# An expert gather ring that runs on over stage boundaries, in a one-core decoder-layer kernel

## The chip, the cores and the metric

The kernel runs on one core of a Trainium2 chip. The metric is the device time of one execution in microseconds. The program is one launch.

## The reference, cut to what matters

One layer of a hybrid decoder for 1104 tokens of 1024 features: 16 learned meta tokens and 1024 prompt tokens in sequence, and 8 samples of 8 tokens that start from given states. All in float32.

```python
h = layer_norm(x)
proj = h @ w_in                     # q, k, v, gates, SSM inputs, two gates z
o = gated_delta_chunked(...)        # 16 heads; a triangular solve in each chunk
y = ssd_chunked(...)                # 16 heads
h1 = layer_norm(ALPHA * h + concat(o, y) @ w_out)
# PEER: for each token, 8 heads pick 16 experts each out of 16384, by two top-16 lists of 128 keys
act = gelu(einsum('thkd,td->thk', u_tab[idx], h1))
ff = einsum('thk,thkd->td', gate * act, v_tab[idx])
y_out = layer_norm(ALPHA * h1 + ff)
```

Every token needs 128 rows of `u_tab` and 128 rows of `v_tab`, 4 KB each. These rows are gathered out of HBM, and they are most of the bytes that the kernel moves.

## The kernel before, in words

**Tiles.** The tokens lie in eight tiles of 128 (tiles 0 to 7) and a last tile of 80 (64 sample tokens and 16 prompt tokens).

**Stages.** The program (L2516) is a series of stages. Each is a block of its own with its own semaphores, and all engines meet in a barrier behind it. A stage of the kind `project` (L130) makes the input projection of two to four tiles; `mix_tile` (L1001) does the two recurrent mixers, the output projection and the choice of experts for one tile. The names here: P1 (tiles 0, 1), M0, M1, P2 (tiles 2 to 4), M2, M3, M4, P3 (tiles 5 to 7 and the last), M5, M6, M7, ML (the last tile), F (the experts of the last tile, `experts_folded`, L2317), and a short stage that stores states.

**The experts run beside the stages.** The work on the experts of tile t is laid over the stages behind Mt. It has two kinds of units. A u unit gathers row n of the choices of all 128 tokens (128 rows of 4 KB, one on each partition, L2122); VectorE multiplies it by the tokens and sums (L2158). A v unit gathers the 128 v rows of one token (L2122 too); TensorE adds them, weighted, to two banks of PSUM, for four tokens at a time with 16 matmuls (L2274), whose weights ScalarE copies into a strip (L2235). When a tile has all of its v units, VectorE normalises it (`normalize`, L2168), and a DMA stores it. `tail` means v units of a tile whose v units began in the stage before, `head` those that begin in this stage after its u units have been turned into weights (`tensor_turn`, L2282). The stages M2 and M5 have no u units: each works off all 128 tokens of tile 1 or of tile 4.

**The ring.** All gathers are issued by GpSimd and land in a ring of 12 slots of 512 KB (`RING`, L783). Slot g mod 12 has one semaphore, `in{g mod 12}`. Before it issues unit g, GpSimd waits until unit g - 12 is used up (`freed`, L2088): a u unit by VectorE's `dot`, a v unit by TensorE's `v_used`, which counts groups of four, a stored tile by its DMA.

**The order.** `order` (L2024) lays the units of a stage over its checkpoints by written weights (`SHARES` L904, `project_points` L118), and every engine works them off at the same checkpoints of its own program. GpSimd runs 12 units ahead. In a mix stage it waits first for two small loads (`consts`, L1137), which SyncE issues fourth and fifth, and casts a mask (L1138); in a project stage it waits for three loads (L276).

**The end of a stage.** Behind its last unit GpSimd waits until every slot has landed, sets `gathered`, and resets the DMA semaphores:

```python
for i in range(RING):
    if self.landings[i]:
        g.wait_ge(S[f"in{i}"], 16 * self.landings[i])
g.sem_inc(S["gathered"], 1)
g.dma_reset(range(min(nums), max(nums) + 1))
```

In a mix stage VectorE waits for `gathered` before it copies the new choices (L2209). The block ends with a barrier; `all_engine_barrier(sems_to_clear=S.range)` is a second one, in which GpSimd clears the semaphores of the stage. The ring and its counts begin at slot 0 again in the next stage. ScalarE takes the strips of the last checkpoint before it computes the softmax's exponentials (L1649 to L1653).

## Time and profile before

| | us |
|---|---|
| median of 3 runs | 4942.41 |
| lowest and highest | 4938.36, 4945.6 |
| profiled execution, first to last instruction (span) | 5061.9 |

For the profiled execution no time is given other than its span, 119.5 us (2.4%) above the median. The stages start at 559.7 (M1), 946.1 (P2), 1332.8 (M2), 1668.1 (M3), 2067.1 (M4), 2509.2 (P3), 2993.0 (M5), 3324.0 (M6), 3720.2 (M7), 4151.5 (ML) and 4796.2 (F) in the span. In rows PE is TensorE, PEld its weight loads, DVE VectorE, ACT ScalarE, POOL GpSimd, SPq the issues of SyncE; `e_ring` is the ring, `e_ff` the two banks of PSUM.

### The profile page before, as it was taken

What the parts mean: (1) busy time and instruction counts of PE and PEld (TensorE: products, weight loads), DVE (VectorE), ACT (ScalarE), POOL (GpSimd) and SP (SyncE); (2) the same over time, 40 slices, a digit from 0 to 9 for tenths busy, and PEclk for the clock granted to TensorE, in tenths of its full rate; (3) what the DMA queues carried; (4) which work ended last, traced back from release to release, by engine and by line L of the source; (5) the groups of instructions that cost most, each with busy time, mean ns of one, the idle gap of its engine ahead of it and who ended that gap; (6) DMA issues with size and microseconds to landing.
All of it is one profiled execution on the core that took longest, in us unless ns stands there. A gap on an engine that the chain in (4) does not pass through costs nothing. (4 is left out here: it accounts for less than half of the span.)

```text
span 5061.9 us, 53189 instructions
## 1 busy us (share of the span) xinstructions
PE 3427.8 (68%) x17745; PEld 1968.4 (39%) x17745; DVE 3195.1 (63%) x7030; ACT 725.4 (14%) x2596; POOL 2650.2 (52%) x2240
## 2 busy tenths in 40 slices
PE   7978377599887576556579988757656564565516
PEld 5666262255462452343144446245234322321101
DVE  5335896588544896677668744489667755664370
ACT  2141110111210210210022121021021011000000
POOL 1000376465435575676546533557567647726564
PEclk9988668699888678776789999877877776677659
DMA  5453478899859789989879875978999988879897
GB/s 180 145 192 119 175 262 327 295 368 353 322 181 366 268 314 369 336 320 335 336 271 355 307 293 167 369 275 307 368 344 321 367 317 300 303 295 361 300 370 281
DMA packets 460478, 1497.56 MB, mean 296 GB/s; under 512 B 53184, under 2 KB 115456, under 8 KB 447632
## 3 DMA queue, kind: packets, MB, share of 16 engines
q0 software_dynamic: 317952, 1141.01, 61.7%
q1 hardware_dynamic: 121040, 330.55, 17.6%
q10 hardware_dynamic: 21216, 22.60, 1.4%
q8 instruction: 145, 2.38, 0.2%
q14 instruction: 125, 1.02, 0.1%
HBM read 1455.22 MB, written 55.52 MB: 298 GB/s over the span
## 5 line engine op out<-in xcount | busy, mean ns | idle before, releaser
L2122 POOL DMA_INDIRECT e_ring<-peer_u,e_idx x1024 | 1325.0, 1294 | 647.9 <-issue 231.6
L2122 POOL DMA_INDIRECT e_ring<-peer_v,e_idxT x1024 | 1119.7, 1093 | 891.4 <-PE e_ff L2274 445.5
L2158 DVE CUSTOM_DVE_ANT_0 e_ring<-e_ring,e_x 128x1024 f32<-128x1024 f32 x1024 | 1226.5, 1234 | 291.1 <-DMA e_ring<-peer_u,e_idx 270.6
L2274 PE MATMUL e_ff<-e_ring,e_strips 128*32 128x512 f32 x4096 | 672.4, 786 | 512.0 <-DMA e_ring<-peer_v,e_idxT 429.5
L352 PE MATMUL p_ps<-p_hT,p_w 128*128 128x256 f32 (+2 forms) x1728 | 569.9, 484 | 0.0
L2274 PEld LDWEIGHTS e_ff<-e_ring,e_strips 128*32 128x32 f32 x4096 | 146.5, 129 | 933.9 <-issue 931.7
L352 PEld LDWEIGHTS p_ps<-p_hT,p_w 128*128 128x128 f32 x1728 | 329.0, 195 | 209.0 <-issue 129.5
L1138 POOL CAST hidden<-delta 128x128 bf16<-128x128 f32 (+1 forms) x9 | 2.9, 317 | 629.7 <-DMA delta<-hidden 605.7
L376 PE MATMUL p_ps<-p_w,p_hT 128*128 128x512 f32 (+1 forms) x576 | 251.2, 599 | 0.0
L1299 PE MATMUL bank<-X,atp 128*128 128x128 f32 (+1 forms) x1120 | 170.5, 304 | 102.3 <-DVE XT L1736 70.7
L1313 PE MATMUL bank<-T,XT 128*128 128x128 f32 (+1 forms) x1088 | 167.8, 304 | 93.1 <-DVE T L1744 91.4
L1911 DVE MAX8 top<-kb_kdec 128x8 f32<-128x128 f32 (+1 forms) x144 | 40.3, 280 | 301.5 <-ACT kb_kdec L1645 248.3
L1504 PE MATMUL bank<-wbuf,kqb 128*128 128x512 f32 (+1 forms) x448 | 209.8, 618 | 0.0
L614 DVE SCALAR_TENSOR_TENSOR p_y<-p_cbuf,p_cw,p_y 128x256 f32<-128x256 f32 (+2 forms) x324 | 198.3, 612 | 11.5
L1299 PEld LDWEIGHTS bank<-X,atp 128*128 128x128 f32 (+1 forms) x1120 | 149.8, 210 | 124.9 <-DVE XT L1736 79.1
L1313 PEld LDWEIGHTS bank<-T,XT 128*128 128x128 f32 (+1 forms) x1088 | 149.6, 214 | 115.6 <-DVE T L1744 101.8
L1322 PE MATMUL bank<-XT,T 128*128 128x128 f32 (+1 forms) x1120 | 160.5, 293 | 3.8 <-DVE T L1744 3.8
L376 PEld LDWEIGHTS p_ps<-p_w,p_hT 128*128 128x128 f32 (+1 forms) x576 | 108.2, 188 | 141.1 <-issue 141.1
L1322 PEld LDWEIGHTS bank<-XT,T 128*128 128x128 f32 (+1 forms) x1120 | 149.7, 210 | 4.2 <-DVE T L1744 4.2
L2235 ACT COPY e_strips<-e_wT 128x4 f32<-128x4 f32 x256 | 48.7, 204 | 688.1 <-PE e_ff L2274 394.8
L1504 PEld LDWEIGHTS bank<-wbuf,kqb 128*128 128x128 f32 (+1 forms) x448 | 83.2, 193 | 136.1 <-issue 135.2
L560 DVE COPY p_tok<-p_ps 128x384 f32<-128x384 f32 (+1 forms) x108 | 55.3, 512 | 118.1 <-PE p_ps L336 109.8
(392 smaller groups left out, 5150.1 us busy)
## 6 DMA issues: line engine op xcount, KB each, us to landing
p_w<-w_in SPq DMA_DIRECT2D x156, 512.0 KB, 3.6
wbuf<-wc SPq DMA_DIRECT2D x56, 1024.0 KB
wbuf<-w_out SPq DMA_DIRECT2D x40, 1024.0 KB
e_ring<-peer_v,e_idxT POOLq DMA_INDIRECT x1104
atp<-w_out SPq DMA_DIRECT2D x16, 1024.0 KB
kb_kdec<-w_out SPq DMA_DIRECT2D x16, 1024.0 KB
atp<-wc SPq DMA_DIRECT2D x16, 1024.0 KB
e_ring<-peer_u,e_idx POOLq DMA_INDIRECT x1024
```

The costliest lines, as they stand in the source:

```text
L352: last = nc.tensor.matmul(ps[j % 2][:, 0:cols], w[:, j % NWR, k, :], hT[:, k, :], start=(k == 0), stop=(k == KT - 1))
L376: last = nc.tensor.matmul(ps[n % 4][0:R, :], hT[:, k, col[i]:col[i] + R], w[:, slot:slot + 4, k, :], start=(k == 0), stop=(k == KT - 1))
L560: last = v.tensor_copy(tok[:, j % 2, 0:nf, :], ps[4 + m % 2][:, 0:prompt].rearrange("p (i n) -> p i n", n=P))
L614: last = v.scalar_tensor_tensor(out=y, in0=xx[:, i:i + convw], scalar=cw[:, j, i:i + 1], in1=y, op0=ALU.mult, op1=ALU.add)
L1299: last = mm(bank[b][0:R, i * P:i * P + R], atp[0:R, s, i, 0, 0:R], X[0:R, s, i, 0:R], start=True, stop=True)
L1313: last = mm(bank[b][0:R, i * P:i * P + R], XT[0:R, s, i, 0:R], T1[0:R, s, i, 0:R], start=True, stop=True)
L1322: last = mm(bank[b][0:R, i * P:i * P + R], T1[0:R, s, i, 0:R], XT[0:R, s, i, 0:R], start=True, stop=True)
L1504: last = mm(bank[2 + i][0:R, :], h1T[:, 4 * half + kk, 0:R], wtile[n + 8][:, kk * 512:(kk + 1) * 512], start=(half == 0 and kk == 0), stop ...
L2122: g.indirect_dma_start(out=self.ring[:, i % RING, :], out_offset=None, in_=table[:, :], in_offset=at, bounds_check=NEXP - 1, oob_is_err=Fa ...
L2158: v.tensor_tensor_reduce(out=self.ring[0:U, i, :], in0=self.ring[0:U, i, :], in1=self.x[0:U, :], scale=1.0, scalar=0.0, op0=ALU.mult, op1= ...
L2235: nc.scalar.copy(self.strips[:, q % NSTRIP, j:j + width, 31:32], self.wT[:, :].rearrange("p (j m) -> p j m", m=32)[:, j:j + width, s:s + 1 ...
L2274: last = nc.tensor.matmul(self.ff[i][32 * j:32 * j + 32, :], self.strips[:, self.strip_of[t] % NSTRIP, j, 31 - s:63 - s], self.ring[:, sel ...
```

## The change

- The ring is one for the whole series of stages. A `Plan` for each stage holds `base`, the number of units before it, and the landings so far of each slot; the semaphores `in0` to `in11` are never cleared between stages, and GpSimd waits no longer for its gathers at the end of a stage. `gathered` is gone.
- At the end of a stage GpSimd issues the first units of the next one, as many as are `known`: v units at the head of its order, at most 12. That is 8 before P2, 12 before M2, 4 before M3, 8 before M4, 12 before P3, 12 before M5, 4 before M6, 8 before M7 and 12 before ML, 80 in all. Each still waits for its slot.
- At the start of a stage GpSimd issues the u units that follow among the first 12 (`fresh`) before it waits for any load.
- The block and the barrier behind it go by semaphores alone, without a drain of GpSimd. SyncE clears the semaphores.
- The weights give a stage with a tail more v units at its very start: in a mix stage at `start`, in a project stage behind the transposes of each tile.
- M2 and M5 take 112 tokens instead of 128. The other 16 are the tail of M3 and of M6, so that tiles 1 and 4 are normalised and stored in the middle of M3 and M6, not at the end of M2 and M5.
- ScalarE does the exponentials before the strips of the last checkpoint.
- Code for an early turn and for a u part in pieces comes in too, and is used by no stage.

```diff
+def stage_end(nc, S):
+    nc.sync.sem_clear(S.range)
+    nc.all_engine_barrier(sem_only=True)
...
-    w = {"ln": (2, 2, 0)}
+    w = {}
+    for i in range(len(tiles)):
+        w["ln", i] = (4, 0, 0)
+    w["ln"] = (0, 2, 0)
...
-        with nc.Block() as block:
+        with nc.Block(no_gpsimd_drain=True) as block:
...
                 if peer:
+                    peer.pool_first(g)
                     at = peer.pool(g)
...
-        nc.all_engine_barrier(sems_to_clear=S.range)
+        stage_end(nc, S)
...
-    "series": {"start": (0, 0, 0), "norm": (0, 0, 0), "prep": (0, 2, 0), "raw": (3, 4, 0), "inv0": (3, 3, 0), "T": (1.6, 2, 0),
+    "series": {"start": (14, 0, 0), "norm": (0, 0, 0), "prep": (0, 2, 0), "raw": (3, 4, 0), "inv0": (3, 3, 0), "T": (1.6, 2, 0),
...
-                for e in range(EH):
+                for e in range(EH - 1):
                     at("best", e)
                 act.wait_ge(S["soft"], 1)
                 nc.scalar.activation(B["best"][0:R], B["best"][0:R], ACT.Exp).then_inc(S["exp_ready"], 1)
+                at("best", EH - 1)
...
+    def slot(self, g):
+        return (self.base + g) % RING
+
+    def known(self):
+        n = 0
+        while n < min(RING, len(self.seq)) and (self.seq[n][0] == "v" and (self.seq[n][1] < self.n_tail or not self.U) or
+                                                self.seq[n][0] == "u" and not self.starts):
+            n += 1
+        return n
+
+    def fresh(self):
+        n = self.known()
+        while n < min(RING, len(self.seq)) and self.seq[n][0] == "u":
+            n += 1
+        return n
...
     def pool_end(self, g):
+        S, p, then = self.S, self.plan, self.then
         self.pool_at()
-        S = self.S
-        for i in range(RING):
-
-            if self.landings[i]:
-                g.wait_ge(S[f"in{i}"], 16 * self.landings[i])
-        g.sem_inc(S["gathered"], 1)
-        nums = [S[f"in{i}"].num for i in range(RING)]
-        g.dma_reset(range(min(nums), max(nums) + 1))
+        if then is None:
+            return
+        for i in range(then.known()):
+            self.freed(g, len(p.seq) + i - RING)
+            self.gather(g, S, then, i)
+
+    def pool_first(self, g):
+        p = self.plan
+        for i in range(p.known() if p.base else 0, p.fresh()):
+            self.gather(g, self.S, p, i)
...
     def take_choice(self, v):
         S = self.S
-        v.wait_ge(S["gathered"], 1)
         self.copy_choice(v, S)
...
-        mix(2, head=(1, 0, P))
-        mix(3, u=2, head=(2, 0, 80))
-        mix(5, head=(4, 0, P))
-        mix(6, u=5, head=(5, 0, 80))
+            (2, dict(head=(1, 0, 112))),
+            (3, dict(tail=(1, 112, P), u=(2, 0, SLOTS), head=(2, 0, 80))),
+            (5, dict(head=(4, 0, 112))),
+            (6, dict(tail=(4, 112, P), u=(5, 0, SLOTS), head=(5, 0, 80))),
```

## Rows read from the trace of the kernel before

**Rows 1.** The page: the span, each engine's busy time, and GpSimd's DMA queue.
```profile
span 5061.9 us, 53189 instructions
PE 3427.8 (68%) x17745; PEld 1968.4 (39%) x17745; DVE 3195.1 (63%) x7030; ACT 725.4 (14%) x2596; POOL 2650.2 (52%) x2240
...
q0 software_dynamic: 317952, 1141.01, 61.7%
```

**Rows 2.** Windows, a stage each: length, then PE, PEld, DVE, ACT, POOL busy (instructions), PEclk, DMA share, GB/s.
```profile
946.10:1332.80 386.70, 334.25 (x1150) 181.91 (x1150) 296.96 (x570) 65.58 (x192) 218.03 (x176) 0.92 0.92 350
1332.80:1668.10 335.30, 250.16 (x1624) 145.67 (x1624) 161.69 (x420) 55.26 (x201) 133.09 (x130) 0.84 0.71 265
1668.10:2067.10 399.00, 259.27 (x1438) 163.88 (x1439) 303.03 (x661) 56.65 (x193) 261.08 (x210) 0.75 0.89 327
2067.10:2509.20 442.10, 278.62 (x1566) 163.59 (x1566) 312.77 (x679) 57.54 (x201) 286.09 (x242) 0.75 0.90 334
2509.20:2993.00 483.80, 413.14 (x1344) 197.04 (x1344) 330.39 (x663) 92.99 (x421) 243.41 (x192) 0.92 0.84 306
...
3324.00:3720.20 396.20, 254.22 (x1438) 159.67 (x1439) 302.84 (x661) 56.16 (x193) 263.88 (x210) 0.77 0.89 329
3720.20:4151.50 431.30, 271.74 (x1566) 158.61 (x1566) 311.74 (x679) 57.55 (x201) 288.07 (x242) 0.77 0.93 342
4151.50:4796.20 644.70, 340.38 (x1950) 147.16 (x1950) 342.01 (x752) 48.45 (x189) 377.87 (x322) 0.69 0.85 312
```

**Rows 3.** Windows around stage boundaries: into P2, into M3, into M5.
```profile
939.10:949.10 10.00, 4.10 (x29) 0.87 (x21) 0.79 (x4) 0.00 (x0) 0.00 (x0) 0.84 0.41 155
...
1650.00:1671.10 21.10, 6.18 (x29) 1.10 (x21) 14.55 (x45) 1.24 (x2) 0.00 (x0) 0.58 0.20 69
...
2957.00:2996.00 39.00, 32.09 (x76) 12.88 (x74) 14.20 (x26) 7.61 (x11) 0.00 (x0) 0.99 0.27 101
```

**Rows 4.** Waits within M4: who for whom, us in total, times, longest.
```profile
PE e_ff L2274 <- DMA e_ring<-peer_v,e_idxT: 52.1, 15, 9.0
```

**Rows 5.** Windows: 60 us of P2 with the DMA engines full.
```profile
1095.00:1155.00 60.00, 58.44 (x228) 32.79 (x227) 56.57 (x110) 11.14 (x40) 41.28 (x35) 1.00 1.03 407
```

**Rows 6.** Timeline, end of M1 and start of P2: start, length, instruction, [idle before, releaser].
```profile
936.31 0.99 POOL L2122 DMA_INDIRECT e_ring<-peer_v,e_idxT  x1 [0.30 <-DMA e_ring<-peer_v,e_idxT]
937.60 3.37 PE L2274 MATMUL e_ff<-e_ring,e_strips 128*32 128x512 f32 x16 [3.55 <-DMA e_ring<-peer_v,e_idxT]
...
942.64 1.92 PE L2274 MATMUL e_ff<-e_ring,e_strips 128*32 128x512 f32 x16 [1.67 <-DMA e_ring<-peer_v,e_idxT]
...
946.12 1.28 SPq L192 DMA_DIRECT2D p_x<-x  x3
...
956.11 0.99 POOL L2122 DMA_INDIRECT e_ring<-peer_u,e_idx  x1 [18.81 <-DMA p_bias<-ln_in_b]
```

**Rows 7.** Timeline, start of M3: the first u unit that VectorE takes.
```profile
1685.76 1.23 DVE L2158 CUSTOM_DVE_ANT_0 e_ring<-e_ring,e_x 128x1024 f32<-128x1024 f32 x1 [8.61 <-DMA e_ring<-peer_u,e_idx]
```

**Rows 8.** Timeline, end of M2 and start of M3.
```profile
1653.44 3.64 PE L2274 MATMUL e_ff<-e_ring,e_strips 128*32 128x512 f32 x16 [1.36 <-DMA e_ring<-peer_v,e_idxT]
...
1657.26 1.29 DVE L2176 BATCH_NORM_STATS2 e_stats<-e_ff 128x6 f32<-128x512 f32 x2
...
1663.67 0.28 DVE L1978 TENSOR_REDUCE norm<-best 128x8 f32<-128x128 f32 x1
...
1665.08 0.22 DVE L2204 COPY e_idxf<-pick 128x128 f32<-128x128 f32 x1
1668.14 0.33 SPq L1071 DMA_DIRECT2D rows<-rows  x1
```

**Rows 9.** Windows, M2, the v matmuls (L2274) alone: length, PE and PEld busy.
```profile
1332.80:1668.10 335.30, 77.98 (x512) 16.88 (x512) 0.84 0.71 265
```

**Rows 10.** DMA issues, size, us to landing: at the start of P3, then amid gathers.
```profile
p_x<-x SPq DMA_DIRECT2D x3, 512.0 KB, 4.6
...
p_x<-x SPq DMA_DIRECT2D x1, 320.0 KB, 6.5
```

More of the change, by code:

```diff
@@ L288, in _ @@
                 ident = B["ident"]
-                if peer:
+                if peer and peer.plan.starts:
                     peer.tensor_start(pe, ps[5])
@@ L482, in _ @@
                 n = Chain(v, S["n_v"])
-                if peer:
+                if peer and peer.plan.starts:
                     peer.vector_start(v, ps[5])
@@ L1481, in _ @@
                 at("turn")
-                if peer.U:
+                if peer.plan.turns and not peer.plan.early:
                     peer.tensor_turn(pe, bank[3])
@@ L1498, in _ @@
                     if half == 0:
-                        if i == 1 and peer.U:
+                        if i == 1 and peer.plan.turns and not peer.plan.early:
                             pe.wait_ge(S["w_taken"], 1)
@@ L1630, in _ @@
                 at("turn")
-                if peer.U:
+                if peer.plan.turns and not peer.plan.early:
                     peer.scalar_turn(act, bank[3])
@@ L1883, in _ @@
                 at("turn")
-                if peer.U:
+                if peer.plan.turns and not peer.plan.early:
                     peer.vector_turn(v)
@@ L2528, in program @@
+        plans, base, counts = [], 0, [0] * RING
+        for some, parts in stages:
+            mixed = None if isinstance(some, list) else some
+            points = project_points(some) if mixed is None else checkpoint_weights("series" if "u" in parts else "tokens")
+            plans.append(Plan(points, base, counts, mixed=mixed, **parts))
+            base, counts = base + len(plans[-1].seq), plans[-1].counts
         project(nc, io, B, [0, 1], pool_dma, consts=Constants(io, B, e))
-        e.B = B
+        e.bind(io, B, None, None)
@@ L2541, in program @@
-        experts_folded(nc, e, pool_dma)
+        for (some, _), plan, then in zip(stages, plans, plans[1:] + [None]):
+            e.bind(io, B, plan, then)
+            if plan.mixed is None:
+                project(nc, io, B, some, pool_dma, peer=e)
+            else:
+                mix_tile(nc, io, B, pool_dma, plan.mixed, e)
+        experts_folded(nc, e, pool_dma, base, counts)
         store_states(nc, io, B)
```

301 lines of the change are left out of this document (164 added, 137 removed).

## The prediction

> **What bounds the kernel now.** I read the page's head first, then windows stage by stage, then windows around the boundaries, then the timeline at three of them.
>
> The page [rows 1] shows no engine at its limit: TensorE is busy for 68% of 5061.9 us, VectorE for 63%. GpSimd's queue, which carries the gathers, moves 1141 MB and takes 61.7% of the 16 DMA engines' time by itself. Stage by stage [rows 2] it is clearer: P2, M3, M4, M6, M7 and ML run the DMA engines at 0.85 to 0.93 while TensorE is busy for two thirds or less (P2 aside). M2 is different, with a share of 0.71 in 335.3 us, and M5 does the same work for its tile. P3 has TensorE at 413 of 483.8 us. In M4 the gathers are what is waited for: TensorE stands 52.1 us before v units [rows 4]. So I call M3, M4, M6, M7 and ML bound by the gathers, M2 and M5 by the tile's own chain, P3 by TensorE, and P2 by both.
>
> The boundaries are where the DMA engines stand still [rows 3]. From the share in each window: into P2 10.0 x 0.59 = 5.9 us, into M3 21.1 x 0.80 = 16.9, into M5 39.0 x 0.73 = 28.5. The other six, read alike, give 9.6 (M2), 7.4 (M4), 7.7 (P3), 16.8 (M6), 5.8 (M7) and 7.3 (ML): 105.9 us in nine. The timeline shows why [rows 6]: GpSimd issues M1's last gather at 936.3, TensorE's last group ends at 944.6, SyncE's first load follows at 946.1 behind the barriers, and the next gather at 956.1, because GpSimd waits for loads first. The stage's end is set by TensorE's last four tokens, not by GpSimd's wait: that wait is over at about 942.7, so its removal alone is worth nothing there.
>
> All terms below are made against the profiled execution (5061.9 us) and taken as microseconds off the median of 4942.4, 2.4% shorter. At this size the difference is below 1 us.
>
> **A: 80 gathers issued before the barriers.** A gather is 128 x 4 KB = 0.524 MB. With the engines full they move 407 GB/s [rows 5], so one costs 1.29 us of DMA time, and 80 cost 103 us. At a boundary this can take no more than the idle time there, nor more than its own gathers: into P2 5.9 us, M3 5.2 (4 gathers), M4 7.4, P3 7.7, M6 5.2, M7 5.8, ML 7.3. Sum 44.5. Into M2 and M5 I count nothing: those stages don't wait for the DMA engines, and P3's end is TensorE's (32.1 us busy of 39 [rows 3]). Its last gather lies far ahead of its end. Into P2 and P3, which TensorE partly bounds, I let the full term stand because the first 8 and 12 tokens now fall where it waits for the layer norm. Bounds: 0, if the stages' own chains take over at once, and 105.9 if every idle microsecond is filled and felt. I take **-44.5**.
>
> **B: u units issued before the stage's loads land.** In M3 VectorE idles 8.6 us before its first u unit [rows 7]; M1 and M6 start alike. GpSimd's first issue moves up by about 10 us, but the stage's loads fill the DMA engines just then. Bounds 0 and 3 x 8.6 = 25.8; I take a third, **-9**, since the transfers still have to share the engines.
>
> **C: no normalisation and no store at the ends of M2 and M5.** VectorE is at 1657.3 when the normalisation begins and at 1663.7 when it is done [rows 8]; the store follows, and M3 starts at 1668.1. Without them the seven short operations from 1663.67 to 1665.30 start at 1657.3 and end at 1658.9. With the 1.6 us that the barriers take from TensorE's last matmul to SyncE's first load [rows 6], the next stage starts at 1660.5: 7.6 us earlier. TensorE's last group ends at 1657.1 and does not hold it. Twice that is **-15.2**, bounds 0 and -16.
>
> **D: 16 tokens from M2 to M3, and from M5 to M6.** M2 gets rid of 64 matmuls at 78.0/512 = 0.152 us [rows 9], 9.8 us of TensorE, and of 8 MB. I take 7 us for each stage, **-14**, bounds 0 and -19.6. M3 and M6 pay. What a token costs in such a stage comes from two pairs [rows 2]: M4 has 32 v units more than M3 and takes 43.1 us longer, M7 has 32 more than M6 and takes 35.1: 1.35 and 1.10 us, a normalisation in the middle included. For 16 tokens 21.6 and 17.5: **+39**, bounds +20 (half, if the new tokens fall into waits) and +43.
>
> **E: GpSimd comes late to the barrier.** A gather takes GpSimd 1.3 us with the gap before it (0.99 and 0.30, [rows 6]). Into P3 and ML the last four of 12 wait for TensorE's last group, so GpSimd is at the barrier 5.2 us behind it. Into P2, M4 and M7 the last four of 8 wait for the group before: at M1's end 941.0 + 5.2 = 946.2, 1.6 us behind TensorE. Together 10.4 + 4.9 = 15.3. What is queued behind the barrier is SyncE's loads and with them the whole next stage, but the DMA engines work meanwhile. Half: **+8**, bounds 0 and +15.3.
>
> **F: the loads of a stage meet gathers.** SyncE's queue is passed by up to 12 gathers. A load of 512 KB at a stage's start lands after 4.6 us, one of 320 KB amid gathers after 6.5 [rows 10], so at least 1.9 us more. Eight stages will begin with gathers in flight: M1, P2, M3, M4, P3, M6, M7 and ML (those for M2 and M5 are released by VectorE's last u units and land before): at 1.9 us 15, if the chain binds. In the gather-bound ones it mostly doesn't: **+4**, bounds 0 and +15 by these rows; how far above it could go is a rival.
>
> **G: the barrier's form.** The clearing moves from GpSimd to SyncE and stays on the path. All of a boundary's sequencing is 1.6 us [rows 6], so twelve of them are worth at most a few microseconds either way: 0, bounds -6 and +6. The earlier exponentials are covered by the last v units, which end later: 0, and 3 us a stage if that cover were gone.
>
> Sum: -44.5 - 9 - 15.2 - 14 + 39 + 8 + 4 = -31.7, which gives **4911 us**.
>
> **Rivals.**
> 1. *All idle DMA time comes back.* If the whole series, M2 and M5 included, is paced by the ring, A is up to -105.9, and with the other terms the change is -93: 4849. For it: shares of 0.9 between the boundaries. Against it: M2's share of 0.71, and P3's end, where nothing waits for a gather.
> 2. *The gain cancels.* The chain of each tile takes over where the gathers were: A falls to -20.5 (only M4, M7 and ML hold), the rest stands: -8, 4935. For it: M3, M6 get work and M2, M5 have room left. The change not doing what it says belongs here: if the new barriers still wait for GpSimd's DMAs, A is gone, and E grows by the flight of 12 gathers.
> 3. *Slower: the loads at the start.* The place is the first 10 us of eight stages, the mechanism the sharing of the DMA engines: 12 gathers are 15.5 us of DMA time, and the rows and gates that a mix stage starts with are 2.4 MB, 6 us. Every microsecond that these land later starts the tile's chain later. From 31.7/8 = 4 us above F's half microsecond on, it decides. At 8 us a stage the change is +28: 4970. For it: 6.5 us for the smaller load [rows 10]. Against it: in gather-bound stages the chain has the slack of its waits [rows 4].
>
> On rival 3 the Trainium skill has a rule (DMA: Bandwidth & Descriptors, Queues, rings and completion order): each DMA engine takes turns between the queues that have work, a packet at a time. By it the 2.4 MB wait for at most as many bytes of gathers, an estimate of 6 us a stage and not 15, and the sum would be about 48 us higher at most, 4955: slower, by the rule's worst case. The rows show 1.9 us and more, and I go by them.
>
> **How the numbers follow.** A measurement of this kernel can tell about 0.2%, 10 us, from no change. The forecast (-10 to -65 us) gets 0.58, rival 1 (beyond -65) 0.14, rival 2 (within 10 us) 0.16, rival 3 0.12. So faster 0.72, same 0.16, slower 0.12. The likeliest case's own range is 4877 to 4932. The range that should hold 8 in 10 goes from 4852, most of rival 1, to 4950, most of rival 2 and the near end of rival 3.
>
> **What would show it.** A: DMA idle at the boundaries into P2, M3, M4, M6, M7 and ML down from 5.8 to 7.7 us to 2 or less, and v matmuls at the start of M4 before the tile's own. B: VectorE's idle before the first u unit of M3 below 6 us. C: M2 and M5 shorter by about 15 us each. D: M3 and M6 no more than 15 us longer than now. E: GpSimd's last gather ends after TensorE's last group at the ends of M4 and M7. F: the first load of M4 lands within 7 us. The forecast is wrong if M4, M7 and ML, which keep their units, don't get shorter by 5 us or more each, or if M2 and M5 stay at 330.

## The result, and the profile after

| | us |
|---|---|
| before, median of 17 runs | 4941.07 (4929.36 to 4950.74) |
| after, median of 17 runs | 4956.71 (4944.22 to 4969.1) |
| ratio after to before | 1.0032, 95% interval 1.0021 to 1.0042 |
| profiled execution of after, span | 4962.1 |

The change makes the kernel slower by 0.32%, 16 us; the forecast was 4911, 32 us faster, and its range ended at 4950.

One warning before the traces are compared. The profiled execution of before (5061.9 us) and the one of after (4962.1) most likely come from different chips: neither carries a chip's number, but stage F, which the change hardly touches, tells them apart. It has 160 gathers of its own; the windows from the issue of its first gather to the issue of its last, before's first and after's second (columns: window, length, PE, PEld, DVE, ACT, POOL busy with instructions, PEclk, DMA share, GB/s):

```profile
4798.20:5029.90 231.70, 90.66 (x355) 25.23 (x352) 97.43 (x166) 5.97 (x39) 158.68 (x160) 0.71 0.95 356
```
```profile
4718.70:4930.50 211.80, 91.04 (x355) 25.34 (x352) 99.61 (x166) 5.98 (x39) 158.73 (x160) 0.72 1.00 391
```

The same gathers take 231.7 us at 356 GB/s on one and 211.8 us at 391 GB/s on the other. So the two spans say nothing about the change, and stage lengths are compared below within chips of one kind: "slow" for chips with this stretch of F at 229 to 240 us, where before takes 5046 to 5064 us, "quick" for those with 212 to 214 us, where it takes 4941.

The page of after, its head and the gather queue, against [rows 1]: work is unchanged, GpSimd issues as much, the queue carries the same 1141.01 MB.

```profile
span 4962.1 us, 53155 instructions
PE 3403.3 (69%) x17745; PEld 1946.6 (39%) x17745; DVE 3194.9 (64%) x7030; ACT 722.8 (15%) x2596; POOL 2665.9 (54%) x2240
...
q0 software_dynamic: 317952, 1141.01, 62.3%
```

The stages of after, in the order P2, M2, M3, M4, P3, M5, M6, M7, same columns, against [rows 2]:

```profile
942.50:1337.10 394.60, 335.35 (x1150) 179.25 (x1150) 296.09 (x570) 65.37 (x192) 221.95 (x181) 0.91 0.92 346
1337.10:1661.10 324.00, 241.43 (x1560) 143.33 (x1560) 155.92 (x402) 54.41 (x197) 108.57 (x107) 0.83 0.64 242
1661.10:2071.10 410.00, 260.62 (x1502) 158.77 (x1502) 309.75 (x679) 56.89 (x197) 289.08 (x230) 0.77 0.92 341
2071.10:2481.00 409.90, 263.73 (x1566) 154.92 (x1566) 310.42 (x679) 57.24 (x201) 286.31 (x244) 0.78 0.96 361
2481.00:2959.60 478.60, 418.81 (x1344) 200.10 (x1344) 330.31 (x663) 92.73 (x421) 244.32 (x196) 0.92 0.88 316
2959.60:3279.10 319.50, 242.53 (x1560) 144.59 (x1561) 155.93 (x402) 54.53 (x198) 108.60 (x106) 0.83 0.63 237
3279.10:3684.10 405.00, 264.18 (x1502) 159.91 (x1503) 309.72 (x679) 56.78 (x198) 285.65 (x230) 0.77 0.93 345
3684.10:4104.20 420.10, 269.94 (x1566) 155.93 (x1566) 310.82 (x679) 57.12 (x201) 291.82 (x245) 0.77 0.95 355
```

M2 and M5 are shorter, and M2's DMA share falls from 0.71 to 0.64; M3 and M6 are longer, even on the quicker chip. Windows at the boundaries into P2, M3, M4, M5 and ML, placed about SyncE's first load as those of [rows 3] are:

```profile
935.50:945.50 10.00, 3.67 (x17) 0.82 (x17) 0.29 (x1) 0.00 (x0) 7.50 (x8) 0.78 1.01 397
1643.00:1664.10 21.10, 6.58 (x33) 1.50 (x33) 16.35 (x47) 1.54 (x4) 1.97 (x2) 0.61 0.24 83
2064.10:2074.10 10.00, 5.58 (x37) 1.27 (x33) 0.29 (x1) 0.30 (x2) 7.46 (x8) 0.83 1.02 383
2923.60:2962.60 39.00, 32.28 (x76) 13.01 (x74) 14.20 (x26) 7.60 (x11) 17.10 (x12) 0.99 0.76 261
4097.20:4107.20 10.00, 4.47 (x21) 0.78 (x17) 0.43 (x2) 0.30 (x2) 6.81 (x7) 0.67 1.02 400
```

This is the puzzle of the case. Into P2, M4 and ML, and just so into P3 and M7, the DMA engines no longer stand still at all: the 5.9, 7.4, 7.7, 5.8 and 7.3 us that the prediction counted have gone, to the microsecond. Into M3 little changed (0.24 against 0.20), into M5 the share rose from 0.27 to 0.76. And yet the kernel is slower.

What the filled boundaries did to the stage behind them stands in the timeline of after at the start of P2, against [rows 6] (start, length, instruction, [idle before, releaser]):

```profile
941.55 0.99 POOL L2169 DMA_INDIRECT e_ring<-peer_v,e_idxT  x1 [0.30 <-issue]
...
942.45 1.28 SPq L201 DMA_DIRECT2D p_x<-x  x3
...
943.18 0.99 POOL L2169 DMA_INDIRECT e_ring<-peer_u,e_idx  x1 [0.65 <-issue]
...
959.48 1.29 DVE L510 BATCH_NORM_STATS2 p_stats<-p_x 128x6 f32<-128x512 f32 x2 [16.35 <-DMA p_bias<-ln_in_b]
```
Before, the same instruction, and that of M4 (next paragraph):
```profile
955.34 1.28 DVE L496 BATCH_NORM_STATS2 p_stats<-p_x 128x6 f32<-128x512 f32 x2 [8.55 <-DMA p_bias<-ln_in_b]
...
2072.41 1.23 DVE L1679 TENSOR_TENSOR kb_kdec<-rows,gt 128x1024 f32<-128x1024 f32 x1 [4.53 <-DMA gt<-gates]
```

From SyncE's first load to VectorE's first layer norm it was 955.34 - 946.12 = 9.2 us; now it is 959.48 - 942.45 = 17.0. In M4 VectorE's first product waits for the gates, 2072.41 - 2067.1 = 5.3 us behind the first load before and 2081.38 - 2071.10 = 10.3 after. The other stages, read alike, are later by 4.9 us (M2), 7.2 (P3), 4.0 (M7) and 4.2 (ML); M3 and M5 not at all, M6 by 1.2:

```profile
2081.38 1.23 DVE L1707 TENSOR_TENSOR kb_kdec<-rows,gt 128x1024 f32<-128x1024 f32 x1 [9.61 <-DMA gt<-gates]
```

And the end of M7, where GpSimd is the last to come to the barrier:

```profile
4090.12 1.92 PE L2340 MATMUL e_ff<-e_ring,e_strips 128*32 128x512 f32 x16 [1.90 <-DMA e_ring<-peer_v,e_idxT]
...
4095.24 3.50 PE L2340 MATMUL e_ff<-e_ring,e_strips 128*32 128x512 f32 x16 [3.20 <-DMA e_ring<-peer_v,e_idxT]
...
4102.26 0.99 POOL L2169 DMA_INDIRECT e_ring<-peer_v,e_idxT  x1 [0.30 <-issue]
...
4104.22 0.32 SPq L1090 DMA_DIRECT2D rows<-rows  x1
```

TensorE's last group ends at 4098.7, GpSimd's last gather of the twelve for ML at 4103.3, SyncE's first load follows at 4104.2, 5.5 us behind TensorE where it was 2.0 before. GpSimd waits for nobody there ([0.30 <-issue]): it is behind with its own issues. At M1's end, with eight gathers to issue, it is 1.0 us behind TensorE, at M4's end, with twelve, 2.6.

The end of M2, against [rows 8]:

```profile
1656.93 1.22 DVE L1980 TENSOR_REDUCE pick<-rows 128x64 f32<-128x1024 f32 x1
...
1659.83 0.22 DVE L2271 COPY e_idxf<-pick 128x128 f32<-128x128 f32 x1
1661.10 0.32 SPq L1090 DMA_DIRECT2D rows<-rows  x1
```

No normalisation and no store stand between the choice and the next stage any more: 1.1 us from VectorE's last copy to the next load, 2.8 before. How much that is shows from an operation that lies before both, VectorE's last write of h in M2, before's first and after's second:

```profile
1546.32 1.28 DVE L1900 SCALAR_TENSOR_TENSOR h<-h,mv,ln_b 128x1024 f32<-128x1024 f32 x1
```
```profile
1551.13 1.28 DVE L1930 SCALAR_TENSOR_TENSOR h<-h,mv,ln_b 128x1024 f32<-128x1024 f32 x1
```

From there to the next stage's first load it was 1668.14 - 1546.32 = 121.8 us and is 1661.10 - 1551.13 = 110.0.

### The profile page after: what moved, and what is told of

Same layout as the page of the kernel before. It is cut to its first block and busy times, and to the rows that moved or that the text cites. A ratio compares the mean times of both kernels' runs of the same rounds, so it can differ in the third digit from the quotient of the medians.

```text
span 4962.1 us, 53155 instructions
## 1 busy us (share of the span) xinstructions
PE 3403.3 (69%) x17745; PEld 1946.6 (39%) x17745; DVE 3194.9 (64%) x7030; ACT 722.8 (15%) x2596; POOL 2665.9 (54%) x2240
## 3 DMA queue, kind: packets, MB, share of 16 engines
q0 software_dynamic: 317952, 1141.01, 62.3%
## 5 line engine op out<-in xcount | busy, mean ns | idle before, releaser
L2169 POOL DMA_INDIRECT e_ring<-peer_v,e_idxT x1024 | 1146.4, 1120 | 883.8 <-PE e_ff L2340 476.5
```

What stands on the lines that cost most here:

```text
L2169: g.indirect_dma_start(out=self.ring[:, plan.slot(i), :], out_offset=None, in_=table[:, :], in_offset=at, bounds_check=NEXP - 1, oob_is_er ...
```

## Experiments

None of these kernels leaves out a part of the computation. Ratios are to the kernel before, timed beside them on the same chip, with 95% intervals. There were five such sets: two on one slow chip, two on two others, one on a quick one. First the whole table; stage lengths are single executions, from one stage's first SyncE load to the next one's.

| kernel | chip | ratio | P2 | M2 | M3 | M5 | M6 | M7 |
|---|---|---|---|---|---|---|---|---|
| before | slow | 1 | 386.7 | 335.3 | 398.9 | 331.1 | 396.1 | 431.4 |
| before_again | slow | (one time) | 383.9 | 336.4 | 393.5 | 333.8 | 393.6 | 430.9 |
| after_again | slow | 0.9987 [0.9969, 1.0005] | 394.2 | 324.2 | 417.9 | 322.7 | 420.9 | 441.8 |
| after_third | slow | 0.9989 [0.9969, 1.0009] | 394.9 | 323.3 | 417.4 | 322.3 | 410.5 | 430.4 |
| barriers | slow | 0.9984 [0.9962, 1.0005] | 386.2 | 335.9 | 395.1 | 336.1 | 398.6 | 434.3 |
| ring_only | slow | 0.9960 [0.9937, 0.9983] | 389.2 | 332.7 | 397.0 | 329.1 | 394.4 | 424.7 |
| full_tiles | slow | 0.9938 [0.9918, 0.9958] | 392.1 | 330.0 | 396.0 | 326.3 | 393.4 | 433.1 |
| full_tiles_b | slow | 0.9946 [0.9926, 0.9967] | 395.1 | 331.9 | 399.1 | 322.5 | 396.9 | 429.3 |
| old_weights | slow | 1.0042 [1.0025, 1.0059] | 389.2 | 325.8 | 419.0 | 322.1 | 414.9 | 439.6 |
| no_ahead | slow | 1.0113 [1.0080, 1.0146] | 389.6 | 328.0 | 426.6 | 331.3 | 430.0 | 433.6 |
| no_first | slow | 0.9991 [0.9971, 1.0011] | 383.4 | 335.7 | 415.0 | 325.8 | 414.1 | 432.3 |
| ahead4 | slow | 1.0021 [1.0003, 1.0039] | 384.6 | 334.2 | 416.0 | 329.4 | 421.6 | 432.7 |
| left_only | slow | 1.0077 [1.0049, 1.0104] | 386.1 | 335.1 | 423.4 | 333.3 | 421.9 | 442.6 |
| left_early | slow | 1.0058 [1.0037, 1.0079] | 386.5 | 325.1 | 423.1 | 329.7 | 422.6 | 427.9 |
| after_early | slow | 0.9984 [0.9967, 1.0001] | 390.6 | 326.1 | 415.6 | 325.1 | 413.7 | 433.5 |
| tuned | slow | 0.9932 [0.9896, 0.9967] | 387.8 | 329.6 | 390.0 | 326.4 | 394.4 | 432.0 |
| tuned_four | slow | 0.9941 [0.9915, 0.9967] | 384.1 | 320.1 | 406.9 | 321.0 | 401.4 | 440.5 |
| after | quick | 1.0032 [1.0021, 1.0042] | 394.7 | 324.0 | 410.0 | 319.4 | 405.0 | 420.2 |
| after_fourth | quick | 1.0018 [1.0005, 1.0030] | 398.5 | 319.3 | 409.9 | 315.2 | 407.7 | 419.1 |
| tuned_again | quick | 0.9964 [0.9951, 0.9977] | 391.6 | 323.8 | 387.6 | 319.8 | 384.6 | 415.6 |

M4 and M7 vary by 10 us and more between executions of one kernel (M4 of before: 442.2 and 421.7; M7 of after: 441.8 and 430.4), so a stage's length there proves little; P2, M2, M3, M5 and M6 repeat within a few microseconds, M6 of after within 10.

### The first four: which part costs

**before_again**, the kernel before once more.

> The kernel before once more, for a second profile. The first one has a span of 5061.9 us, 120 us above the median of the times, while the profile of the changed kernel has 4962.1, at its median. If the first profile is an odd one, this span is near 4940, and the stages that are shorter than in the first profile tell where the odd 120 us lay; if profiling the kernel before always costs 2.4%, the span is near 5060 again and stages can be compared as they are.

One time, 5018.33 us, the lowest of before on the slow chips. Neither reading of its expectation is right: the profile costs nothing (23 executions beside it have a median of 5045.73), and the odd 120 us are most likely the chip.

**full_tiles**: the change with 128 tokens in M2 and M5 and no tails in M3 and M6.

```diff
-            (2, dict(head=(1, 0, 112))),
-            (3, dict(tail=(1, 112, P), u=(2, 0, SLOTS), head=(2, 0, 80))),
+            (2, dict(head=(1, 0, P))),
+            (3, dict(u=(2, 0, SLOTS), head=(2, 0, 80))),
```
(The same for M5 and M6.)

> The changed kernel with 128 tokens in M2 and M5 again, and no tail in M3 and M6; the ring, the barriers and the weights stay. Theory 1 (the moved tokens eat the gain: they cost 39 us in M3 and M6 and give back less than the 29 us forecast): 4930 or less, below the kernel before. Theory 2 (the loads at a stage's start land late behind gathers): about 4950, as the changed kernel, for the head starts of the other stages remain. Theory 3 (the new weights at the start disturb the tile's chain): about 4950 too.

5012.76 us against 5045.73: 0.9938 [0.9918, 0.9958]. Without the leftover tokens the change gains 31 us, as its first theory says. It also issues no gathers ahead into M3 and M6, which have no tail then: 72 of the 80 are left.

**old_weights**: the change with the weights of before.

```diff
-    for i in range(len(tiles)):
-        w["ln", i] = (4, 0, 0)
-    w["ln"] = (0, 2, 0)
+        w["ln", i] = (0, 0, 0)
+    w["ln"] = (2, 2, 0)
...
-    "series": {"start": (14, 0, 0), ...
+    "series": {"start": (0, 0, 0), ...
```

> The changed kernel with the old weights: no v units ahead of the others in P2, M4, P3, M7 and ML, so the only units known before a barrier are the 12 of M2 and of M5; the u units at the starts are still issued early. Theory 3 (weights disturb): 4940 or less. Theory 1 and 2: head starts of M4, M7 and ML lost, 4960 to 4975 by theory 1; below 4950 by theory 2 in so far as fewer gathers meet the loads.

1.0042: against after_again, which comes below, the new weights are worth 28 us, and between ring_only and full_tiles, both without leftover tokens, 7 to 11. They are not the cause. What they change is more than the order: with the old ones only 28 gathers are known before a barrier (12 each into M2 and M5, 4 into P3), so these two differences come nearest to the prediction's term A.

**no_ahead**: the change, but GpSimd issues nothing before a barrier or before a load.

```diff
-        while n < min(RING, len(self.seq)) and (self.seq[n][0] == "v" and
+        while n < 0 and (self.seq[n][0] == "v" and
...
-        while n < min(RING, len(self.seq)) and self.seq[n][0] == "u":
+        while n < 0 and self.seq[n][0] == "u":
```

> The changed kernel without any gather issued before a barrier or before a stage's loads; barriers, ring numbering, weights and the 16 moved tokens stay. Theory 1: the head starts are worth 30 to 50 us, so 4985 to 5005. Theory 2: the head starts cost what they bring or more, so 4930 to 4960. Theory 3: between, 4960 to 4975.

1.0113, 57 us, as the first theory says (4985 to 5005 is 0.9 to 1.3% above before's 4941). The new weights put TensorE's first v units ahead of the tile's own work, so without gathers in flight TensorE stands before them: its first transposes in M3 and M6 came 27.3 and 28.5 us behind the stage's start, 9.2 and 9.4 in after_again. Head start and weights belong together.

### The change again, and how far GpSimd should run ahead

**after_again**, the change itself beside these.

> The changed kernel once more. It and the kernel before were measured at 4957 and 4941 us; in the first set of experiments the kernel before took 5046, so chips differ by 2%, and the variant with 128 tokens in M2 and M5 came out 0.6% faster than before there. Theory 1 (the moved tokens cost 0.9%): on any chip this is 0.2 to 0.4% slower than the kernel before. Theory 4 (the worth of the ring that runs on depends on the chip: where gathers are slower, head starts are worth more): 0.3% slower on a chip with 4940, but at least 0.3% faster on one with 5040.

0.9987: on this chip no difference that can be told, where the result says 1.0032. The two intervals do not meet. Neither theory forecast that: one said 0.2 to 0.4% slower on any chip, the other at least 0.3% faster on this one. The section on the chip comes back to it.

**full_tiles_b**, as full_tiles, beside it.

> 128 tokens in M2 and M5, otherwise the changed kernel, beside the changed kernel itself. Theory 1: 0.6% faster than before on any chip, 40 us faster than the changed kernel. Theory 4: within 10 us of the changed kernel.

0.9946, by the medians 24.7 us below after_again and by the ratios 21; the intervals do not meet. The theory had said 40.

**no_first**: the u units wait behind GpSimd's loads as before; gathers before the barrier stay.

```diff
-        while n < min(RING, len(self.seq)) and self.seq[n][0] == "u":
+        while n < 0 and self.seq[n][0] == "u":
```

> The changed kernel, but u units at a stage's start are issued behind the wait for loads, as before; those issued before the barrier stay. Theory 2 (gathers in front of a stage's loads delay the tile's chain): the chain starts of P2, M4, M7 and ML come back in part from 5 to 8 us late, and the time falls by 5 to 20 us against the changed kernel. If my term B is right instead, it rises by about 9.

0.9991: the early u units are worth nothing in sum, neither the 5 to 20 us against them nor the 9 for them. But P2 tells what they do: 383.4 us instead of 394.2, with the layer norm 962.91 - 952.76 = 10.1 us behind the first load instead of 16.7, though the eight gathers before the barrier are still there. In this execution it is given back elsewhere (M2 is 11 us longer). M2, M4, P3, M7 and ML start as late as in the change (M4: 10.7 us).

```profile
962.91 1.29 DVE L510 BATCH_NORM_STATS2 p_stats<-p_x 128x6 f32<-128x512 f32 x2 [9.33 <-DMA p_bias<-ln_in_b]
```

**ahead4**: besides that, at most four gathers before a barrier.

```diff
-        while n < min(RING, len(self.seq)) and (self.seq[n][0] == "v" and
+        while n < min(4, len(self.seq)) and (self.seq[n][0] == "v" and
```

> As no_first, and at most 4 gathers are issued before a barrier instead of 12. Theory 2: the loads of P2, M2, M4, P3, M7 and ML land at their old times (first VectorE operation of M4 at 5.5 us instead of 10.3), GpSimd is never late at a barrier, and the time is 10 to 30 us below the changed kernel. If head starts are worth their DMA time (my term A), 56 gathers fewer are missed and it is 20 to 40 us above.

1.0021, 17 us above after_again by the ratios (the intervals just meet). The loads are used at their old times again, P2's layer norm at 9.3 us, M4's first product at 5.4:

```profile
2085.77 1.23 DVE L1707 TENSOR_TENSOR kb_kdec<-rows,gt 128x1024 f32<-128x1024 f32 x1 [4.71 <-DMA gt<-gates]
```

And the kernel is no faster for it, let alone by the 10 to 30 us of theory 2: fewer gathers ahead cost at least what the late loads do. With no_first this tells the two kinds of stage apart. In M4 and the other mix stages the gathers before the barrier hold the loads: eight do, four do not. In P2 it is mostly the u units issued beside the loads: 16.7 us with eight gathers ahead and four u units, 10.1 with the eight alone, 12.2 in ring_only with two u units and none ahead. Each is a single execution.

### One part at a time

**left_only**: the kernel before, with only the tokens moved.

```diff
-        mix(2, head=(1, 0, P))
-        mix(3, u=2, head=(2, 0, 80))
+        mix(2, head=(1, 0, 112))
+        mix(3, tail=(1, 112, P), u=2, head=(2, 0, 80))
```
(The same for M5 and M6.)

> The kernel before with one part of the change: M2 and M5 take 112 tokens, 16 are the tail of M3 and M6; ring, barriers, weights as before. Theory 1 with the terms as the traces now show them (in M3 and M6 16 tokens cost 20 to 27 us each; in M2 and M5 the missing store and tokens give back 7 to 11 each): 25 to 35 us slower than before, 0.5 to 0.7%. By the forecast's terms C and D (-15.2 - 14 + 39): 10 us slower, 0.2%.

1.0077, 39 us slower than before by the ratio, where the theory said 25 to 35 and the prediction's C and D 10. M3 and M6 are 29.8 and 28.3 us longer than in before_again, and M2 and M5 are 1.3 and 0.5 shorter.

**ring_only**: full_tiles with the old weights. **barriers**: that, and nothing issued ahead, so that the barriers' form, the numbering of the ring, the missing wait for landings and the earlier exponentials are left.

> 128 tokens in M2 and M5 and the old weights, with the new ring and barriers: before a barrier only the 12 units of M2 and of M5 are issued, and u units early at the starts of M1, P2, M3 and the others. If the front-loaded weights carry the gain of the variant with full tiles (0.6%), this is within 0.2% of before; if the ring does, it is 0.3 to 0.6% faster.

> As the last one, but with no gather issued before a barrier or before a stage's loads: what is left of the change is the form of the barriers, the numbering of the ring, no wait for the last landings, and the earlier exponentials. Forecast (term G): within 6 us of before. If the wait for GpSimd's DMAs had cost something at the ends that the timeline did not show: more than 10 us faster.

0.9960 and 0.9984. ring_only still issues 28 gathers before barriers, into M2, M5 and P3, and the early u units; the prediction had counted M2 and M5 as nothing. So on slow chips, each by its ratio: barriers -8 us (interval -19 to +3), these gathers -12 more, the weights with the gathers into P2, P3, M4, M7 and ML that they make known 7 to 11 more, and the leftover tokens +21 (after_again less full_tiles_b). Of the single steps only the last is clear of the noise. From barriers to full_tiles, the whole head start, it is -23 (to full_tiles_b -19).

**tuned**: full_tiles with at most eight gathers before a mix stage and four before a project stage, at most six u units before the loads of a mix stage and none in a project stage.

```diff
-        while n < min(RING, len(self.seq)) and (self.seq[n][0] == "v" and
+        while n < min(8 if self.mixed is not None else 4, len(self.seq)) and (self.seq[n][0] == "v" and
...
-        while n < min(RING, len(self.seq)) and self.seq[n][0] == "u":
+        while n < min(6 if self.mixed is not None else 0, len(self.seq)) and self.seq[n][0] == "u":
```

> Full tiles and new weights, but fewer gathers in the way: at most 8 before a barrier into a mix stage and 4 before one into a project stage, at most 6 units before the mask's cast in a mix stage and none before a project stage's loads. Theory 2 (late loads and a late GpSimd give the gain back): P2's layer norm starts below 11 us again instead of 17, M7's last v group is followed by the next load within 4 us instead of 8, and the time is 10 to 30 us below the variant with full tiles, 0.8 to 1.1% faster than before. If these delays are hidden, the two are within 10 us.

0.9932 [0.9896, 0.9967], the lowest ratio of all, not told apart from full_tiles: of the two forecasts the second, that these delays are hidden, holds. P2's layer norm is at 11.0 us, M7's last v group is followed by the next load within 3.8.

### Why M2 and M5 gave nothing back

In left_only the chain of M2 itself runs late. Two stretches of M2, 88 to 104 and 126 to 160 us behind its start, in before_again, left_only and left_early (same columns as above):

```profile
1419.53:1435.53 16.00, 13.13 (x99) 11.07 (x98) 12.15 (x22) 0.00 (x0) 4.19 (x4) 0.89 0.53 183
1457.53:1491.53 34.00, 28.47 (x183) 20.89 (x183) 11.21 (x25) 8.36 (x28) 11.28 (x11) 0.75 0.65 219
```
```profile
1418.45:1434.45 16.00, 12.22 (x76) 9.99 (x76) 10.52 (x18) 0.00 (x0) 4.17 (x4) 0.79 0.54 183
1456.45:1490.45 34.00, 29.79 (x229) 22.30 (x223) 8.38 (x22) 9.25 (x31) 6.95 (x7) 0.60 0.47 157
```
```profile
1422.18:1438.18 16.00, 13.13 (x97) 11.07 (x96) 11.75 (x19) 0.00 (x0) 4.19 (x4) 0.89 0.48 164
1460.18:1494.18 34.00, 29.56 (x194) 22.33 (x195) 13.03 (x27) 8.03 (x27) 12.12 (x12) 0.80 0.71 243
```

With 112 tokens the written weights lay the units at other checkpoints: fewer matmuls in the first stretch, and in the second TensorE's granted clock, 0.75 in before_again, is 0.60: between the levels 1.2 and 2.4 GHz that is four fifths of the stretch at the lower one. In the 22 us before it TensorE had been busy for 20.7 at a granted clock of 1.00. In M5 the same stretch has 0.80 in before_again and 0.60 in left_only. The last write of h comes at 222.4 and 221.9 us of M2 and M5 instead of 214.6 and 212.0. left_early lays the 112 where the first 112 of 128 lay:

```diff
-                to = min(size[i], unit[i] * int(round(size[i] * so_far[i] / total[i] / unit[i])))
+                lay = P if i == 2 and size[i] == 112 else size[i]
+                to = min(size[i], unit[i] * int(round(lay * so_far[i] / total[i] / unit[i])))
```

> The kernel before with 112 tokens in M2 and M5 and the tails of 16 in M3 and M6, as in left_only, but the 112 lie at exactly the checkpoints where the first 112 of 128 lay before; what is missing is missing at the end of the stage. Nothing of the computation is left out. Theory (placement and clock): in left_only the v matmuls that used to lie between 88 and 104 us of M2 were laid elsewhere, TensorE's granted clock in the following 34 us was 0.60 against 0.75 in the second execution of before, and the tile's chain ran 8 us late. By it the last write of h comes at 214 to 216 us of M2 again (222.4 in left_only, 214.6 before), the clock of 126 to 160 us is 0.75 or more, M2 and M5 take 322 to 328 us (335.1 and 333.3 in left_only), and the ratio to before is 1.003 to 1.006. Rival (the chain runs late with 112 tokens wherever they lie, or the end of the stage is set by something that the normalisation covered): M2 and M5 stay at 332 or more and the ratio at 1.0075.

The matmuls of the first stretch (76, now 97) and the clock of the second (0.80) are back. M2 is 325.1 us (left_only 335.1), M5 329.7 (333.3), 11.3 and 4.1 less than before_again, 7.7 on average: about the 7.6 of term C, and nothing for the 16 tokens. 1.0058 is 10 us below left_only by the ratios, but the two intervals overlap. M5 got its clock back only in part (0.75; h is written at 215.6 us, in M2 at 211.4). So the placement moved the chain of M2 in these single executions, and half that of M5; that it does so by way of the clock goes with the rows, but is not shown.

**after_early**: the same placement in the changed kernel.

> The changed kernel with the same placement of M2's and M5's 112 tokens as in left_early. Nothing is left out. Theory: h at 205 to 209 us as with 128 tokens (211.3 and 212.1 in after_again), M2 and M5 317 to 321 us (324.2 and 322.7), 8 us off the changed kernel: ratio to before 0.996 to 0.998. Rival: M2 and M5 stay within 2 us of after_again, ratio 0.9985 to 1.000.

A miss: 0.9984 against after_third's 0.9989, M2 and M5 at 326.1 and 325.1 us against 323.3 and 322.3. There VectorE's choice of experts ended at 323.2 us of M2, 110.8 behind h, and the stage 2.9 behind that. h came at 212.4 us, no earlier than in after_again (211.3), so the placement is not what holds h there. And TensorE's last group ended 28 us before the stage did, where in after_again it is 3: the end of M2 is the choice's, whatever TensorE does.

**tuned_four**: tuned with 124 tokens in M2 and M5 instead of 128, so that only four are left over.

```diff
-            (2, dict(head=(1, 0, P))),
-            (3, dict(u=(2, 0, SLOTS), head=(2, 0, 80))),
+            (2, dict(head=(1, 0, 124))),
+            (3, dict(tail=(1, 124, P), u=(2, 0, SLOTS), head=(2, 0, 80))),
```

> The version tuned (at most 8 v units ahead into a mix stage and 4 into a project stage, at most 6 early u units, none in a project stage), but with 124 tokens in M2 and M5 and 4 left over instead of 128, placed as the first 124 of 128. It keeps the part C of the prediction (no normalisation and store at the ends) and a quarter of D. Theory: M2 and M5 each 7 us shorter than tuned (329.6 and 326.4), M3 and M6 each 4 x 1.5 = 6 us longer (390.0 and 394.4) plus up to 3 for the normalisation in their middle: from 2 us below tuned to 4 above, ratio to before 0.993 to 0.9945. Rival (the cost of a tail is mostly fixed, its second set of strips and its normalisation, not per token): M3 and M6 15 us longer or more, ratio 0.996 or above.

M2 and M5 are 9.5 and 5.4 us shorter than in tuned, as C says. M3 and M6 are 16.9 and 7.0 longer, the one as the rival says and the other as the theory: on average 12 for four tokens. With 16 tokens they are 20 longer (M3 and M6 of after_again and after_third, mean 416.7, against full_tiles and full_tiles_b, 396.4). These two means give an estimate of 9 us for having a tail at all and 0.7 for each token; with a scatter of 10 us behind the first of them neither figure is firm. The whole is a draw: 0.9941 and 0.9932.

### The chip

> The changed kernel once more, in the same company as the three above. If this chip moves the gathers of stage F at 356 GB/s as in the other experiments, the ratio is 0.9987 within 0.0018; if at 387 GB/s as in the profile of the changed kernel, 1.002 to 1.004.

It was a slow chip again (F: 231.6 us), and the ratio, 0.9989, came as forecast.

> The changed kernel on one more chip. If stage F's 160 gathers take 229 to 236 us from the first issue to the last landing, as on the three chips of the other experiments, the ratio is 0.9987 within 0.0018. If they take 212 us, as in the first profile of the changed kernel, the ratio is 1.002 to 1.004, and before itself takes about 4941 us.

> The version tuned beside it. On a chip with slow gathers 0.993 within 0.003. On one with fast gathers two theories part: if the head start is worth in proportion to the DMA time that it saves, the ratio is 0.994 to 0.997; if fast gathers take its whole worth away, 0.999 to 1.001.

This set had a quick chip: before took 4940.58 us. The change is slower there again, 1.0018 [1.0005, 1.0030], and tuned faster, 0.9964 [0.9951, 0.9977], 28 us below the change. F's window of tuned_again and, behind it, of after_third:

```profile
4666.30:4878.30 212.00, 86.64 (x355) 24.53 (x352) 99.76 (x166) 5.98 (x39) 158.70 (x160) 0.73 1.00 390
```
```profile
4770.70:5002.30 231.60, 95.50 (x355) 25.94 (x352) 97.19 (x166) 5.98 (x39) 158.22 (x160) 0.70 0.96 357
```

M3 and M6 on the quick chip, without a tail in tuned_again and with 16 tokens in after_fourth, are 22.2 and 23.1 us apart:

```profile
1646.30:2033.90 387.60, 253.96 (x1438) 159.98 (x1438) 302.75 (x661) 56.24 (x193) 269.94 (x218) 0.79 0.92 342
...
3244.40:3629.00 384.60, 253.47 (x1438) 160.16 (x1438) 302.58 (x661) 56.33 (x193) 266.50 (x218) 0.77 0.93 346
```
```profile
1659.20:2069.00 409.80, 267.84 (x1502) 163.88 (x1502) 309.83 (x679) 56.82 (x197) 277.88 (x230) 0.75 0.93 341
...
3270.70:3678.40 407.70, 258.39 (x1502) 156.27 (x1502) 310.03 (x679) 56.62 (x197) 279.02 (x229) 0.77 0.92 341
```

So the leftover costs about as much on both kinds, and the gain of the head start is what shrinks: tuned is worth 0.68% on a slow chip and 0.36% on a quick one (the intervals, 0.33 to 1.04% and 0.23 to 0.49%, overlap, so this is likely, not shown). For the change the two kinds differ: 1.0032 [1.0021, 1.0042] and 1.0018 [1.0005, 1.0030] on quick ones, 0.9987 [0.9969, 1.0005] and 0.9989 [0.9969, 1.0009] on slow ones; the first of the quick ones is clear of both, the second touches them.

## Why the prediction was wrong

The sum had two halves: -41.5 us for the head start (A, B, E, F, G) and +9.8 for the tokens (C, D). Measured on slow chips: full_tiles, which is the first half with the weights but without the eight gathers into M3 and M6, is -31 and -27; the second half is +21, and the change -6 in all. On a quick chip tuned, the only form of the first half that was run there, is -18, the tokens 27 more, and the change +9 in that set, +16 in the result. Two steps failed, and the sign needed both: with one of them as forecast the kernel would have come out 8 or 14 us faster. The first is A, which took idle time at a boundary for time of the kernel. The second is D's -14, the time that M2 and M5 were to give back for the 16 tokens.

- **A, -44.5: the idle time went, the time did not.** Five of the seven boundaries were filled, 34.1 of 44.5 us. Into M3 the share stayed at 0.24: VectorE's choice of experts ends the stage there, and the four gathers for M3 had been issued 19 us before its start. Of the 34.1 us, 7 to 11 came back from ring_only to full_tiles and 28 from old_weights to after_again, each with an interval of 10 us and more to either side. P3 was 7 us shorter on slow chips (mean 481.6 to 474.4) and ML 11 (640.7 to 629.6), but P2 9 us longer. The claim that P2 would profit because TensorE idles before the layer norm was wrong in its direction: the layer norm itself moved.
- **F, +4: the loads do come late, by half a microsecond counted and 4 to 8 measured.** 7.8 us in P2, 7.2 in P3, 5.0 in M4, 4.2 in ML, 4.0 in M7, and 4.9 in M2, for which the prediction had expected nothing; M3 and M5 are spared. That is rival 3's mechanism, and near its point of decision, 4 us in each of eight stages. It did not decide: ahead4 has all six back at their old times and is no faster, and only P2's length follows its loads (-10 us in no_first and ahead4). The Trainium skill's rule (DMA: Bandwidth & Descriptors, Queues, rings and completion order: a DMA engine takes turns between its queues packet by packet) had given at most 6 us a stage as an estimate. The trace agrees in the four mix stages, with 4.0 to 5.0 us; P2 and P3 lie above it. It was a better guide than the 1.9 us of [rows 10], which came from a load of another size in another traffic.
- **B, -9: nil.** VectorE's idle before its first u unit of M3 fell from 8.6 to 1.1 us, as the test asked. But GpSimd now casts the mask that the tile's chain needs behind its gathers: at 13.0 us of M3, and at 17.6 in full_tiles, where 12 u units go first, against 8.8 before. By the ratios the early u units are worth nothing (no_first 0.9991, after_again 0.9987).
- **E, +8: right in place and about in size.** The prediction let GpSimd come 5.2 us behind TensorE into P3 and ML and 1.6 into P2, M4 and M7; in after it is 2.6, 4.5, 1.0, 0.9 and 0.7. From TensorE's last group to the next load M7's end takes 3.5 us more than before and M4's 1.4. P2's end, which the prediction left out, takes 1.9 more: there too twelve gathers are issued.
- **G, 0: -8 at best** (-19 to +3), beyond the bound of -6 that was set. The rows allow that much: in barriers TensorE's last matmul ends 0.9 us before the next load at the boundaries into P2, M2, M4, M7 and ML, where before it was 1.4 to 2.0.
- **C, -15.2: right.** From the last write of h to the next stage M2 and M5 take 120 to 122 us in before and full_tiles and 109 to 113 in the change, somewhat more than the 7.6 us less. That little of it shows in the change's stages (they are 4.6 us shorter on average than in full_tiles) is D's doing.
- **D, -14: nothing, and in M5 less than nothing.** M2's end is VectorE's choice of experts, a chain of its own behind h, and TensorE's 9.8 us lay beside it, as the prediction itself said of TensorE's last group; it still let 7 us stand for each stage. What counts is whether h comes earlier, and it does not: against full_tiles and full_tiles_b it comes 1 us later in M2 (mean 209.9 to 210.7) and 8 us later in M5 (203.1 to 211.1), in left_only 8 and 10 later than in before_again.
- **D, +39: 35 to 46 in the change, 58 in left_only, so right in size, by luck.** The price came from M4 less M3 in one execution, 43.1 us; in before_again the same difference is 28.1, and it holds M4's tail and its tokens in one figure.
- **The 2.4%.** The prediction saw a profile 119.5 us longer than the median and wrote that it changed the terms by less than 1 us. It was most likely another chip, with gathers 9% slower: every wait for a gather in it, and every gain from issuing gathers earlier, was read from a slower chip than the one that was timed.

Of the tests that the prediction set, A's was met into P2, M4, M7 and ML and not into M3 and M6; B's and E's were met, and C's came out at 12.1 and 10.0 us of the 15 (slow chips, means of M2 and M5). D's (no more than 15 us; 20 and more) and F's (M4's chain) were not. Of its signs of being wrong, one showed: M7 is no shorter on slow chips (431.2 to 436.1, with 11 us between two executions of after), M4 2 us (432.0 to 429.9, with 20 between two of before), ML 11. Tests of a cause were met while the time went the other way, because they asked for the idle time and not for the stage's length.

**What stays open.** Why A's microseconds did not come back in M4 and M7 could not be read from those stages, whose length varies by more than the term. How the 27 us of the tokens on the quick chip divide is open too: tuned differs from the change in its caps as well. That gathers' speed alone decides the difference between chips is not shown either; the two kinds may differ in more.

**A better version than both** is tuned: 5024.85 against 5062.78 us on a slow chip and 4921.07 against 4940.58 on a quick one, -0.36% [-0.49, -0.23].

## What to carry to other kernels

An idle resource at a boundary is worth only what the next stage's start can take: before counting it, ask which loads will queue behind the work that fills it, and cap the head start by them. Price work that moves between stages in both places by what ends each stage: in the giving one it is worth nothing if another engine's chain sets the end, and in the receiving one measure the piece itself, because a difference between two large stages holds their scatter and more than one cost. When the profile's span and the timed median differ by more than the runs' spread, find a stretch that does the same work in every kernel and compare it before taking microseconds from one to the other.

## What the runs showed of the hardware

- Chips differ in how fast they gather: from the issue of the first to that of the last, the same 160 gathers of 0.524 MB took 229 to 240 us on three chips and 212 to 214 us in three executions of which two came from one chip, with the DMA engines busy for about 0.95 of the time on the former and 0.99 to 1.00 on the latter. The whole kernel differs by 2.4% between them, and a change that costs 0.2 to 0.3% on the one costs nothing that can be told on the other.
- With the v matmuls of 112 tokens instead of 128 in M2, laid anew, TensorE's granted clock was 0.60 instead of 0.75 over 34 us, in M5 0.60 instead of 0.80; with the 112 laid as before it was 0.80 and 0.75, and M2 10 us shorter. It is one execution of each; that a lighter stage can get a slower clock had not been in the prediction.
- Eight to twelve gathers issued before a barrier had the first loads of a mix stage used 4.0 to 5.0 us later, though twelve are 15.5 us of DMA time; four gathers delayed them by nothing (M4: 5.4 us in ahead4, 5.3 before), and so did M5's twelve, all issued 8 us before its first load.
- A stage's end by semaphores alone took 0.9 us from TensorE's last matmul to SyncE's first load (barriers, into P2, M2, M4, M7 and ML), and 1.4 to 2.0 with a drain of GpSimd and its clearing of the semaphores (before).
